# Gate vectors of a second block: from matmuls with the identity to a store and a broadcast load

## The reference, cut to what matters

```python
mod = silu(c) @ ada_w[i] + ada_b[i]
sh1, sc1, g1, sh2, sc2, g2 = split(mod, 6)         # 1024 channels each; the same for c_ctx: cg1, cg2
y, yc = mixer(modulate(x, ...), modulate(ctx, ...))  # i = 0: attention, i = 1: state space, x only
x = x + g1 * y
x = x + g2 * swiglu(modulate(x, ...), ...)
if not last:
    ctx = ctx + cg1 * yc
    ctx = ctx + cg2 * swiglu(modulate(ctx, ...), ...)
```

## Time and profile before

| | |
|---|---|
| time, median of 3 runs | 2637.03 us (2635.67 to 2637.7) |
| span of the profiled execution (the page gives no other time of it) | 2636.9 us |
| TensorE busy | 98% of the span |
| VectorE / ScalarE / GpSimd busy | 54% / 20% / 12% |
| TensorE's mean granted clock | 0.989 of full speed |
| DMA | 129 GB/s mean, 252,563 packets |

### The profile page before, as it was taken

The page is one execution under the profiler, slowest core; times in us unless marked ns, Lnnn a source line. Parts: engine busy times, 40 slices in busy tenths (PEclk is TensorE's granted clock), DMA queues, the critical chain, the costliest instruction groups (busy, mean ns, idle before and its releaser), DMA issues.

```text
span 2636.9 us, 38612 instructions
## 1 busy us (share of the span) xinstructions
PE 2577.2 (98%) x16192; PEld 1999.4 (76%) x16192; DVE 1427.3 (54%) x2632; ACT 533.7 (20%) x1249; POOL 316.0 (12%) x367
## 2 busy tenths in 40 slices
PE   8999999999999999999999999999998999999998
PEld 7889886874688888778458656888886566666997
DVE  1575434865436554375345834555433468864775
ACT  1342111100025121111011742000002244321100
POOL 2002110320100111032000000000000134520110
PEclk9999999999999999999999899999999999999999
DMA  7341113787633211368762002222222343334553
GB/s 260 113 127 50 38 45 128 265 282 253 203 121 112 87 44 34 128 222 272 270 223 80 17 26 71 86 90 81 88 88 68 112 146 119 121 99 149 169 171 108
DMA packets 252563, 340.76 MB, mean 129 GB/s; under 512 B 7236, under 2 KB 178372, under 8 KB 252264
## 3 DMA queue, kind: packets, MB, share of 16 engines
q1 hardware_dynamic: 240592, 310.66, 36.3%
q10 hardware_dynamic: 8920, 17.67, 2.0%
q0 software_dynamic: 2880, 9.96, 1.1%
HBM read 337.08 MB, written 1.19 MB: 128 GB/s over the span
## 4 chain that ended last, share of the span: by engine, by line
PE 93%; DVE 2%; DMA 2%; issue 1%; ACT 1%; POOL 0%; ACTq 0%; SPq 0%; POOLq 0%; DVEq 0%
PE PS L995 17%; PE PS L397 13%; PE PS L443 9%; PE PS L669 6%; PE PS L1250 6%; PE PS L783 5%; PE PS L1037 5%; PE PS L974 4%; PE PS L682 3%; PE PS L1083 2%; PE PS L1227 2%; PE PS L435 2%; PE PS L749 1%; PE PS L407 1%; PE PS L558 1%
## 5 line engine op out<-in xcount | busy, mean ns | idle before, releaser
L995 PE MATMUL PS<-MEM 128*128 128x256 f32 (+1 forms) x2632 | 447.5, 332 | 0.7 <-DVE MEM L2394 0.7
L995 PEld LDWEIGHTS PS<-MEM 128*128 128x128 f32 x2632 | 407.0, 190 | 40.8 <-DVE MEM L2394 0.9
L397 PE MATMUL PS<-MEM 128*128 128x256 f32 x1632 | 358.2, 381 | 5.6 <-DMA MEM<-w_up 5.6
L1353 ACT ACTIVATE MEM<-PS 128x256 f32<-128x256 f32 (+4 forms) x405 | 168.3, 428 | 956.7 <-PE PS L397 229.0
L397 PEld LDWEIGHTS PS<-MEM 128*128 128x128 f32 x1632 | 310.0, 191 | 48.9 <-DMA MEM<-w_up 6.4
L443 PE MATMUL PS<-MEM 128*128 128x512 f32 x608 | 263.4, 594 | 5.8 <-POOL MEM L2874 2.8
L1956 DVE SCALAR_TENSOR_TENSOR MEM<-MEM 128x512 f32<-128x512 f32 x280 | 218.9, 815 | 60.6 <-DMA MEM<-ada_w 54.7
L443 PEld LDWEIGHTS PS<-MEM 128*128 128x128 f32 x608 | 115.0, 190 | 150.3 <-issue 140.4
L2824 POOL TENSOR_TENSOR MEM<-MEM 128x1 f32<-128x1 f32 (+1 forms) x34 | 21.8, 643 | 1273.3 <-DVE MEM L1902 816.3
L669 PE MATMUL PS<-MEM 128*128 128x256 f32 x768 | 172.3, 382 | 0.0
L1250 PE MATMUL PS<-MEM 128*128 128x512 f32 (+1 forms) x512 | 170.4, 485 | 0.0
(11 more groups left out here) (377 smaller groups left out, 3325.5 us busy)
## 6 DMA issues: line engine op xcount, KB each, us to landing
MEM<-w_in SPq DMA_DIRECT2D x54, 1024.0 KB, 5.4
MEM<-ada_w SPq DMA_DIRECT2D x48, 1024.0 KB, 7.4
MEM<-w_up SPq DMA_DIRECT2D x32, 1024.0 KB, 5.4
MEM<-w_down SPq DMA_DIRECT2D x32, 1024.0 KB, 5.2
MEM<-ssm_w_in SPq DMA_DIRECT2D x24, 1024.0 KB, 5.4
MEM<-ffn_gate SPq DMA_DIRECT2D x22, 1024.0 KB, 5.3
MEM<-ffn_up SPq DMA_DIRECT2D x22, 1024.0 KB, 5.3
MEM<-ffn_down SPq DMA_DIRECT2D x20, 1024.0 KB, 5.0
```

Source lines behind the costliest of these rows:

```text
L397: ins = pe.matmul(bank[:, 0:T], W[:, k, c * P:(c + 1) * P], XT[:, k, :], start=k == 0, stop=k == KT - 1)
L995: ins = pe.matmul(out, left[:, k, :], right[:, k, :], start=k == 0, stop=k == 3)
L1353: act.activation(out, view(b), func, **kw).then_inc(S("bank_read_by_act"), 1)
```

## The change

The six gate vectors are stored to a tensor in memory, `gate_dram` (6 x 1024), by six DMAs that ScalarE issues after the four V copies of n = 0. Each writes 1024 single floats: partition p writes its eight numbers 128 floats apart. GpSimd then waits for the stores and loads each gate for n = 0 to 3 with a broadcast load of 512 KB to GR, when the residual before has read the old one. VectorE waits for these loads (`gates_loaded`) where it waited for the copies. The 48 matmuls (96 records) and the 12 copies are gone.

```diff
-            def gate_rows(n, l, which, streams):
-                pe.wait_ge(S("mods_ready" if l else "gains_ready"), 1)
-                for t in range(streams):
-                    for half in range(2):
-                        bank = take(("gr", n, t, half), "act")
-                        for k in range(4):
-                            g = MODF[:, l, t, which, 4 * half + k:4 * half + k + 1].to_broadcast([P, P])
-                            ins = pe.matmul(bank[:, k * P:(k + 1) * P], g, ident, start=True, stop=True)
-                        done(ins)
...
-                    gate_rows(n, l, 5, 2 - l)
...
-                    gate_rows(0, 0, 2, 2)
...
-            gate_rows(2, 1, 2, 1)
...
-            gate_rows(0, 2)
             modulated(0, (0,))
             for t in range(NT):
                 copy(("v2", t), VV[:, t, :], lambda b: b[:, 0:T])
+            act.wait_ge(S("mods_ready"), 1)
+            for r, (l, t, which) in enumerate(GATE_ROWS):
+                act.dma_start(io["gate_dram"][r].rearrange("(k p) -> p k", p=P), MODF[:, l, t, which, :],
+                              allow_slow_non_contiguous=True).then_inc(S("gates_stored"), 16)
...
-                            emptied(dve, ("gr", n, tiles // NT - 1, 1))
+                            dve.wait_ge(S("gates_loaded"), 16 * GATES_LOADED[n])
...
+            def gates_loaded(n):
+
+                pool.wait_ge(S("gates_stored"), 16 * len(GATE_ROWS))
+                if n:
+                    pool.wait_ge(S("x_tiled"), max(v for (m, _), v in tiled_at.items() if m == n))
+                for r, (l, t, which) in enumerate(GATE_ROWS):
+                    if (l, which) == (n // 2, 2 + 3 * (n % 2)):
+                        pool.dma_start(GR[:, t, :], io["gate_dram"][r].partition_broadcast(P)).then_inc(S("gates_loaded"), 16)
+
             for n in range(3):
                 for t in RMS_TILES[n][0 if n else NT:]:
                     power(MS2[:, t:t + 1])
+                gates_loaded(n)
...
             for t in RMS_TILES[3]:
                 power(MS2[:, t:t + 1])
+            gates_loaded(3)
             pool.dma_start(GR[:, 1, :], io["final_g"].partition_broadcast(P)).then_inc(S("gain_loaded"), 16)
```

More of the change, by code:

```diff
@@ L336, in build @@
         tiled_at = {(1, 0): 1, (1, 1): 2, (1, 2): 3, (1, 3): 4, (2, 2): 5, (2, 3): 5, (2, 0): 6, (2, 1): 6, (3, 0): 7, (3, 1): 8, (4, 0): 9, (4, 1): 10}
+        GATE_ROWS = [(0, 0, 2), (0, 1, 2), (0, 0, 5), (0, 1, 5), (1, 0, 2), (1, 0, 5)]
+        GATES_LOADED = (2, 4, 5, 6)
         ada_at = {}
@@ L1098, in gate_by_tile @@
                 later = normed_banks(1)
-                rows = [take(("gr", 3, 0, half), "act") for half in range(2)]
                 W = a_slab(io["ffn_gate"][l], 0)
@@ L1112, in gate_by_tile @@
                 turn_normed_tile(3, 1, later)
[L1113 to L1117, removed]
                 for half in range(2):
@@ L1378, in squares2 @@
                     act.activation(XN[:, t, :], tile2(t), ACT.Square, accum_out=MS2[:, t:t + 1]).then_inc(S("tile_squared"), 1)
[L1380 to L1383, removed]
             def modulated(n, which=None):
@@ L1611, in feed_forward_sevens @@
                     squares2(n, (3,))
-                    gate_rows(n, 2)
                     modulated(n, (1,))
@@ L1619, in feed_forward_sevens @@
                     modulated_tile(1)
-                    gate_rows(n, 1)
                 for f in range(2):
@@ L1705, in _ @@
             squares2(2)
-            gate_rows(2, 1)
             modulated(2)
@@ L2499, in narrow_joined @@
                         settle()
-                        emptied(dve, ("gr", n, 0, 1))
+                        dve.wait_ge(S("gates_loaded"), 16 * GATES_LOADED[n])
                         b = filled(dve, "dve", ("n", 2, half))
@@ L2571, in down_joined @@
                         settle()
-                        emptied(dve, ("gr", n, 1, 1))
+                        dve.wait_ge(S("gates_loaded"), 16 * GATES_LOADED[n])
                         link(scaled(DA1, 0, ca))
@@ L3067 @@
     io["ecf_dram"] = nc.dram_tensor("ecf_dram", (64, T), F32, kind="Internal").ap()
+    io["gate_dram"] = nc.dram_tensor("gate_dram", (6, D), F32, kind="Internal").ap()
     io["out"] = nc.dram_tensor("out", (1, T, D), F32, kind="ExternalOutput").ap()
```

## The result

The changed kernel takes 2643.06 us (median of 12 runs, 2640.06 to 2652.05) against 2636.34 us (2630.48 to 2638.86) for the kernel before beside it: the ratio is 1.0033, with a 95% interval of 1.0024 to 1.0043, or 6.3 to 11.3 us (1.0033 is the quotient of the two means; that of the medians is 1.0025). It is slower, and by more than the 0.2% that I had called measurable. The forecast of 2634.6 named the wrong side; the time lies inside the range, between the upper end of rival B (2642) and rival C (2648).

The account below looks back on a forecast made before the run. TensorE, busy 98% of the span, was taken as the bound. -3.6 (n = 0) + 1.2 (clock at n = 1) + 0 = -2.4 on the 2636.9 span, 0.1 below the median, gave 2634.6 us; range 2632.5 to 2647.

Parts of the forecast that it names:

- rival B: At n = 0 the stores queue up a little and `p1` comes late: 2640.1, between 2635.6 and 2642; chance 0.27.
- rival C: At n = 0 the store issues drain as slowly as the slabs at the start: +10.9, 2648 us; chance 0.22.
- the four places: Removing gate matmuls gains 3.57 us at n = 0 and 0 at n = 1, 2 and 3.
- GpSimd's waits and loads: Waiting for the stores and loading gates at n = 0 to 3 costs 0 each.
- The 5.9 us that ScalarE has before TensorE waits: At n = 0, time for the six store issues between the last V copy and TensorE needing `p1`: 5.9 us.
- the price of the six stores: On ScalarE's list at n = 0: issues of 3.6 us, hidden, so cost 0; upper bound 17.2 us, 11.3 TensorE's.
- the slab issues at the start: SyncE's first four weight-slab issues took 9.27 us together, longest 3.995; basis for the stores' upper bound at n = 0.
- the clock at n = 1: TensorE's longer idle at n = 1 lowers its clock, three chances in four: +1.2 us, bounds 0 and 2.25.
- exposed stores: Rival C's term at n = 0: of 17.2 us of store issues, 11.3 us are TensorE's wait.
- clock behind them: Rival C's term for TensorE's slower clock after the wait for the stores at n = 0: +2.0 us.
- A: The forecast: stores hidden at n = 0, 2634.6 us (2633.3 without the clock's fall, 2635.6 with the dearest); chance 0.45.
- The threshold of 12.5 us for the six issues: At n = 0, the kernel becomes measurably slower once the six store issues take over about 12.5 us.

Follow-up runs that it names:

- Experiment 5: Kernel before plus six DMAs of 1024 words each ahead of the first `p1`: stores with words 64 bytes apart (issues 6.3 us), or loads instead (6.8 us).

## Why the prediction was wrong, point by point

**Right:** the four places. n = 0 gave 3.56 us (forecast 3.57); n = 1, 2 and 3 gave none of their 7.5 us of TensorE work, and the waits became 4.30 and 8.03 (forecast 4.3 and 8.2). The variant that loads only at n = 0 shows it from the other side: 1259.9 against 1260.2. GpSimd's waits and loads cost nothing. The 5.9 us that ScalarE has before TensorE waits was nearly right: three profiles (15.51 - 9.11, 12.27 - 5.87, 6.80 - 0.40) give 6.40. Most of the 0.5 is that the issues began with the last V copy (1386.17 and 1386.18) and not behind it, as I had put them.

**The step that failed** is the price of the six stores. I had bounded it by 3.6 us (the store row of 0.606 each) and 17.2 us (the slab issues at the start), and took the lower value, a cost of 0, because "four bytes should drain faster than 1 KB". It was 15.5 us, of which TensorE waited 9.1, and it was 12 to 15 us in four other kernels: the drain of 1024 pieces was slower than that of a slab, not faster. The nearest row in bytes was the wrong neighbour; the sentence set against it, that writing memory in such small pieces may be slow in itself, was the one to price. Experiment 5 says what is slow: neighbouring words written singly. The same number of pieces 64 bytes apart took 6.3 us: more than my 3.6, but with no wait.

The rule of the Trainium skill that I weighed ("DMA: Bandwidth & Descriptors", section "Rules for kernel authors": a strided last dimension lowers to one descriptor per element, make it contiguous) spoke against the change and pointed the right way: 32-byte runs cut the six issues from 15.5 to 2.9 us. It gives no time, and it does not tell the two stores of 1024 single words apart that differ here by a factor of two in their issues (12.3 against 6.3 us) and of nearly three in landing (18.2 against 6.6).

**A term that was mis-sized** is the clock at n = 1: +1.2 forecast, with an upper bound of 2.25; it measured 3.4 us in the change, 3.4 to 3.9 in its variants. The sign and the cause were right. I bounded the work at half clock by the 4.5 us that followed the idle of n = 2, but here TensorE was still at 0.50 until 1618, 5 us after its restart at 1612.95, and in part of the stretch behind that: the turning lost 1.7 us, and the products behind it 1.7. The 1.0 for the turning was a misreading of mine: only 4.5 of the 5.90 us at n = 2 were at half clock. And the trace of before held a longer case, 11.18 us of work at 0.50 behind 1464.70, which should have set the bound.

**Rival C** was what happened in the second block. Its terms, with the measured ones behind them: n = 0 -3.6 (-3.6), clock at n = 1 +1.2 (+3.4), exposed stores 11.3 (9.1), clock behind them 2.0 (2.2). Its sum of +10.9 stands against +9.6 in the second part, or +10.7 without before's 1.1; that the parts come so close is in part luck, since the misses of the second and third term cancel. It had 0.22 of the chance, and should have had more than A: the upper bound came from the only rows in which SyncE issued a burst of so many pieces, which was the change's own situation. The threshold of 12.5 us for the six issues was passed. (The kernel with the stores alone, at 12.3, does not test it, since it has not the gain at n = 0.)

## What to carry to other kernels

Price a DMA by its pieces and where they land, not by its bytes: a 4 KB store of single neighbouring words took 11 to 20 us to land, and behind three of them, issued in 3.3 us, the next three took 11.3. Whatever is issued from a compute engine's list belongs behind the item that the bottleneck waits for; one moved loop was worth 10.6 us here. And before taking work out of a bottleneck engine, ask whether it stood in a shadow: there it is worth nothing, and it may be what keeps the engine's clock up: 16 hidden matmuls taken out cost 3.4 us at n = 1.

## What the hardware showed that I had not expected

- Six stores of 1024 single words: 12.3 to 15.5 us of issue time from ScalarE when the words are neighbours in memory, 6.3 us when they lie 64 bytes apart, 2.9 us as runs of 32 bytes; six loads of as many words 6.8 us.
- The same stores issued by GpSimd took 0.89 us each and did not block it, with the same time to landing (median 16.3 us).
- An idle of 4.3 us ahead of the turning was followed by 0.50 of the clock in every kernel in which it was left open, five of five, and by 1.00 in every one where 16 matmuls filled it, used or unused.
- At the start of the attention, behind an idle of 2.97 us, every profile shows 0.50 for a while, but for different lengths, and it costs 1.1 us more in two of nine (223.8 against 222.7 us for the same work).
